# The recurrence's inputs, gate and value products moved beside the differential attention, with x loaded twice

## What is computed

```python
proj = x @ w_in            # columns a_q, a_f, a_i, a_g (512 each), b_q, b_k, b_v (512 each)
o_a = _hgrn2(a_q, a_f, a_i, lb)                 # 4 heads; scores (from q, f) times the inputs i
o_a = _rms_norm(o_a, hgrn_g) * silu(a_g)        # norm and gate of the recurrence
o_b = diff_attention(b_q, b_k, b_v, lam)        # 4 heads, (softmax(Q1K1') - lam softmax(Q2K2')) V
o_b = _rms_norm(o_b, diff_g) * (1.0 - lam_init)
x = LN(alpha * x + concat([o_a, o_b]) @ w_out)  # then SwiGLU; layer 1 is forgetting attention
```

## Time and profile before

| | us |
|---|---|
| median of 3 runs (lowest, highest) | 1513.64 (1512.14, 1517.49) |
| the profiled execution: its time | 1518.29 |
| the profiled execution: span, first to last instruction | 1516.5 |
| mean granted TensorE clock, share of full speed | 0.961 |
| PE busy | 1414.4 |
| DVE, ACT, POOL busy | 491.5, 499.5, 495.9 |

### The profile page before, as it was taken

One profiled execution on the slowest core, in us unless ns is written; L12 is line 12 of the kernel. 1 busy time (PEld: TensorE's weight loads), 2 busy tenths in 40 slices (PEclk: granted clock), 3 DMA queues, 4 the chain that ended last, 5 costly groups with the idle time before them and its releaser, 6 DMA issues.

```text
span 1516.5 us, 18942 instructions
## 1 busy us (share of the span) xinstructions
PE 1414.4 (93%) x7212; PEld 1182.7 (78%) x7212; DVE 491.5 (32%) x1120; ACT 499.5 (33%) x824; POOL 495.9 (33%) x213
## 2 busy tenths in 40 slices
PE   7999996798999999999989998889899999999997
PEld 5888874578888888877878887777679888888875
DVE  3366526554111111013636272542362111110105
ACT  4312335423323222112435554444423232322120
POOL 4421312033443535341242222202133344445340
PEclk9999997999999999999999999889899999999999
DMA  6211121021323233221232121012112323323211
GB/s 215 87 53 56 56 84 55 1 84 57 111 84 111 83 98 111 97 84 30 84 111 57 57 57 56 1 55 83 31 56 84 109 86 103 92 90 118 95 59 56
DMA packets 136322, 117.44 MB, mean 77 GB/s; under 512 B 5412, under 2 KB 112036, under 8 KB 136232
## 3 DMA queue, kind: packets, MB, share of 16 engines
q1 hardware_dynamic: 136232, 116.23, 24.6%
HBM read 114.12 MB, written 2.10 MB: 77 GB/s over the span
## 4 chain that ended last, share of the span: by engine, by line
PE 81%; DVE 8%; ACT 6%; issue 3%; DMA 1%; POOL 0%; ACTq 0%; POOLq 0%; DVEq 0%; SPq 0%
PE banks L448 24%; PE banks L450 23%; PE banks L449 23%; PE banks L851 2%; PE banks L869 2%; ACT w_hi L966 1%; PE banks L715 1%; PE banks L519 1%; ACT p_fox L1188 1%; PE banks L860 1%; DVE fox_ms L1496 1%; PE banks L815 1%; DVE o_even L1366 1%; DVE xT_lo L1240 1%; DVE small L1400 1%
## 5 line engine op out<-in xcount | busy, mean ns | idle before, releaser
L926 POOL TENSOR_TENSOR w_lo<-w_raw,w_hi 128x1024 fp32r<-128x1024 f32 (+1 forms) x209 | 495.7, 2393 | 983.9 <-ACT w_hi L966 983.9
L448 PE MATMUL banks<-xT_lo,w_hi 128*128 128x512 f32 (+2 forms) x912 | 345.4, 379 | 5.0 <-DVEq L1242 5.0
L449 PE MATMUL banks<-xT_hi,w_lo 128*128 128x512 f32 (+2 forms) x912 | 342.8, 376 | 0.0
L450 PE MATMUL banks<-xT_hi,w_hi 128*128 128x512 f32 (+2 forms) x912 | 342.7, 376 | 0.0
L966 ACT ACTIVATE w_hi<-w_raw 128x2048 fp32r<-128x2048 f32 (+1 forms) x107 | 200.0, 1869 | 215.5 <-PE banks L450 177.8
L448 PE MATMUL banks<-w_lo,xT_hi 128*128 128x512 f32 (+1 forms) x608 | 222.8, 366 | 9.9 <-issue 5.8
L450 PE MATMUL banks<-w_hi,xT_hi 128*128 128x512 f32 (+1 forms) x608 | 215.6, 355 | 0.0
L449 PE MATMUL banks<-w_hi,xT_lo 128*128 128x512 f32 (+1 forms) x608 | 215.3, 354 | 0.0
L448 PEld LDWEIGHTS banks<-xT_lo,w_hi 128*128 128x128 f32 (+1 forms) x912 | 173.1, 190 | 35.9 <-issue 5.8
L449 PEld LDWEIGHTS banks<-xT_hi,w_lo 128*128 128x128 f32 (+1 forms) x912 | 173.3, 190 | 30.4
L450 PEld LDWEIGHTS banks<-xT_hi,w_hi 128*128 128x128 f32 (+1 forms) x912 | 173.0, 190 | 30.7
(11 more groups left out here) (167 smaller groups left out, 1293.7 us busy)
## 6 DMA issues: line engine op xcount, KB each, us to landing
w_raw<-in_ffn_w_dram SPq DMA_DIRECT2D x92, 512.0 KB, 4.5
w_raw<-in_ffn_w_dram SPq DMA_DIRECT2D x20, 1024.0 KB, 4.9
w_raw<-in_fox_w_in_dram SPq DMA_DIRECT2D x16, 1024.0 KB, 5.8
w_raw<-in_even_w_in_dram SPq DMA_DIRECT2D x14, 1024.0 KB, 5.0
w_raw<-in_even_w_out_dram SPq DMA_DIRECT2D x4, 1024.0 KB, 5.0
w_raw<-in_fox_w_out_dram SPq DMA_DIRECT2D x4, 1024.0 KB, 6.7
x_res<-in_x_dram SPq DMA_DIRECT2D x4, 512.0 KB, 7.6
out_dram<-x_res SPq DMA_DIRECT2D x4, 512.0 KB, 2.6
```

The source lines that it names most:

```text
L448: mm(acc, l_hi, r_lo, start=first, stop=False)
L449: mm(acc, l_lo, r_hi, start=False, stop=False)
L450: return mm(acc, l_hi, r_hi, start=False, stop=final)
L926: ins = nc.gpsimd.tensor_tensor(w_lo[c % RING][:, a:a + n], w_raw[c % RAW][:, a:a + n], w_hi[c % RING][:, a:a + n].bitcast(F32), ALU.subtract)
```

## The change

The stage a_i leaves the mixed stretch, which keeps 24 pieces (b_q, b_k, b_v) and 40 units; the chunks of a_i are loaded after those of b_v. In the attention stretch 20 fillers stand in 16 slots: the 8 pieces of a_i, the value products of the 4 heads, the 8 pieces of a_g, filler k in slot k * 16 // 20. So a_i is in slots 0 to 5, the value products in slots 6, 7, 8 and 8, a_g in slots 9 to 15; slots 0, 4, 8 and 12 have two. The gate moves to slot 16, the turning to slot 18, and first_out behind the last slot. scT now holds all four heads. iv and a_gate lie in x_res, so x is loaded a second time (4 DMAs of 512 KB), ahead of the weights of out0[3], after all gate products.

```diff
-        mixed = [(c, p) for s in ("a_i", "b_q", "b_k", "b_v") for c in stage_chunks[s] for p in range(PIECES)]
+        mixed = [(c, p) for s in ("b_q", "b_k", "b_v") for c in stage_chunks[s] for p in range(PIECES)]
...
-        scT, e = take("scT", [2, 10, P], F32, e)
-        iv, e = take("iv", [NT, 512], F32, e)
+        scT, e = take("scT", [AH, 10, P], F32, e)
...
+        early = x_res[:, :, :].rearrange("p t n -> p (t n)").rearrange("p (a t n) -> p a t n", a=2, t=NT)
+        iv, a_gate = early[:, 0], early[:, 1]
...
-        gate_pieces = [(c, p) for c in stage_chunks["a_g"] for p in range(PIECES)]
-        GATE_AT = len(gate_pieces) + 1
-        TURN_AT = GATE_AT + 4
+        fillers = [("piece", c, p) for c in stage_chunks["a_i"] for p in range(PIECES)]
+        fillers += [("value", h, 0) for h in range(AH)]
+        fillers += [("piece", c, p) for c in stage_chunks["a_g"] for p in range(PIECES)]
+        FILL_SLOTS = D_UNITS
+        def fillers_at(s):
+            return [x for k, x in enumerate(fillers) if k * FILL_SLOTS // len(fillers) == s]
+        GATE_AT = FILL_SLOTS
+        TURN_AT = GATE_AT + 2
...   PE, slot s
+                for kind, a, b in fillers_at(s):
+                    if kind == "value":
+                        value_products(a)          # waits merge_done of the head and i_done, 4
+                    else:
+                        next(late[chunks[a][0]], None)
-                if TURN_AT + 2 <= s < TURN_AT + 2 + NT:
-                    next(first_out)
+                if s == TURN_AT:
+                    for t in range(NT):
+                        turn_tile("o0", t, o_even, lambda: pe.wait_ge(S["gated"], t + 1), t, (0,))
...   PE, behind the last slot
+            for t in range(NT):
+                pe.wait_ge(T_hi, 2 * NT + t + 1)
+                pe.wait_ge(T_lo, 2 * NT + t + 1)
+                next(first_out)
...   SP
+                if c == stage_chunks["out0"][3]:
+                    bank, count, _ = uses[("value", AH - 1)]
+                    sp.wait_ge(bank_full[bank], count)
+                    sp.wait_ge(S["gated"], NT)
+                    for t in range(NT):
+                        sp.dma_start(x_res[:, t, :], x[:, t, :]).then_inc(x_in[t], 16)
...   ACT, slot s, ahead of the exponentials
+                for kind, a, b in fillers_at(s - 1):
+                    if kind == "value":
+                        value_act(a)               # one evacuation, four squares
+                        continue
+                    if chunks[a][0] == "a_i" and a == stage_chunks["a_i"][1]:
+                        evac(("a_i", b), iv[:, b, :], whole)
+                        act.sem_inc(S["i_done"], 1)
+                    if b == 1 or b == PIECES - 1:
+                        hi_upto(a + 3 if b == 1 else a + 4)
+                for kind, a, b in fillers_at(s - 3):
+                    if kind == "value":
+                        root(stats[:, :, 16 + a], stats[:, :, 8 + a], S["var_hgrn"], a + 1, S["root_hgrn"])
...   ACT, slot s, behind the copy of unit s-2
+                if s == GATE_AT:
+                    for t in range(NT):
+                        evac(("a_g", t), a_gate[:, t, :], whole, ACT.Silu)
+                    act.sem_inc(S["gate_done"], 1)
+                    nc.scalar.preload_act_table_set(LN_EXP)
...   DVE, slot s, behind norm_head of the attention
+                for kind, h, _ in fillers_at(s - 2):
+                    if kind == "value":
+                        norm_var(h, 0)
+                for kind, h, _ in fillers_at(s - 4):
+                    if kind == "value":
+                        norm_head(h, 0)
+                if s == GATE_AT + 1:
+                    dve.wait_ge(S["gate_done"], 1)
+                    for t in range(NT):
+                        chain(tt(o_even[:, t, 0:512], o_even[:, t, 0:512], a_gate[:, t, :], ALU.mult), S["gated"])
```

More of the change, by code:

```diff
@@ L108, in weight_chunks @@
     columns("b_v", we, 3072)
+    columns("a_i", we, 1024)
     columns("a_g", we, 1536)
@@ L703, in unit_products @@
                 if kind in MM:
-                    acc = open_bank(("unit", u), 4 + nth((*MM, "value"), u) % 4, "dve")
+                    acc = open_bank(("unit", u), 4 + nth(MM, u) % 4, "dve")
                     pe.wait_ge(S["decayed"], nth(MM, u) + 1)
@@ L743, in _ @@
                 if stage not in pieces:
[L744 removed]
+                    if stage == "b_v":
                         pieces[stage] = columns(stage, "act")
@@ L749, in _ @@
                 next(pieces[stage], None)
-            for stage in ("a_i", "b_q", "b_k", "b_v"):
+            for stage in ("b_q", "b_k", "b_v"):
                 drain(pieces[stage])
@@ L778, in _ @@
                     n = (i + 1) * P
-                    maps = [open_bank(("score", s, m), (0 if wide and s % 2 else 4) + m, "act") for m in range(2)]
+                    maps = [open_bank(("score", s, m), 4 + m, "act") for m in range(2)]
                     for m, acc in enumerate(maps):
@@ L1010, in _, with value_act @@
             nc.scalar.preload_act_table_set(LN_EXP)
[L1012 to L1023 removed]
+            def value_act(h):
+                acc = full(("value", h))
+                release(fn(o_even[:, :, h * P:(h + 1) * P], acc[:, :].rearrange("p (t n) -> p t n", t=NT),
+                           ACT.Copy), ("value", h))
+                for t in range(NT):
+                    chain(fn(junk[:, :], o_even[:, t, h * P:(h + 1) * P], ACT.Square,
+                             accum_out=stats[:, t, 8 + h:9 + h]), S["ms_hgrn"] if t == NT - 1 else act_step)
             due = []
@@ L1373, in _ @@
                     merge(u - 2)
-                if u >= 6 and units[u - 6][0] == "value":
-                    norm_head(units[u - 6][1], 0)
             dve.sem_inc(S["act_free"], 1)
@@ L1415, in _ @@
                     norm_head(u // NT, 1)
-                if GATE_AT + 1 <= s <= GATE_AT + NT:
-                    t = s - GATE_AT - 1
-                    dve.wait_ge(S["gate_done"], 1)
-                    chain(tt(o_even[:, t, 0:512], o_even[:, t, 0:512], a_gate[:, t, :], ALU.mult), S["gated"])
+                for kind, h, _ in fillers_at(s - 2):
[5 more added lines that the diff above has]
+                if s == GATE_AT + 1:
+                    dve.wait_ge(S["gate_done"], 1)
+                    for t in range(NT):
+                        chain(tt(o_even[:, t, 0:512], o_even[:, t, 0:512], a_gate[:, t, :], ALU.mult), S["gated"])
+                if s == TURN_AT + 1:
+                    for t in range(NT):
+                        split_lo("o0", t, (0,))
             dve.sem_inc(S["o_ready"], NT)
             def add_left(key, t, half):
+                if key[0] == "out0" and half == 0:
+                    dve.wait_ge(x_in[t], 32)
                 xs = x_res[:, t, half * 512:(half + 1) * 512]
```

116 lines of the change are left out of this document (38 added, 78 removed).

## The result

| | before | after |
|---|---|---|
| median of 16 runs each (lowest, highest), us | 1514.63 (1510.2, 1517.68) | 1522.75 (1518.04, 1525.2) |
| the profiled execution: its time | 1518.29 | 1518.48 |
| its span | 1516.5 | 1516.7 |

The ratio is 1.0046, 95% interval 1.0035 to 1.0056: slower, where 1508.4 and faster were forecast, and outside the range of 1498 to 1520. Times are medians, and one kernel's runs spread over some 7 us. Two later sets of runs of the same kernel gave 1.0027 (1.0015 to 1.004) and 1.0035 (1.0023 to 1.0047). The two profiled executions are of nearly the same length only because that of before was among the longest of its kernel and that of after among the shortest; the stretches must be compared one by one.

The account below looks back on a forecast made before the run. PE was taken as the bound, busy 1414.4 of 1516.5 us, so a change gains only where PE waits. Terms -34.1 + 11.9 + 17.0 = -5.2 took the median 1513.6 to 1508.4 us, range 1498 to 1520.

Parts of the forecast that it names:

- the clock: Attention stretch: matmuls slowed by a lower granted clock, counted as 3 us in all.
- Mixed stretch: First unit to first filler: 8 pieces (22.9), 4 value products (8.6) and a wait (2.6) go, 34.1 us less.
- the wait of 3.18: Mixed stretch: PE's wait for DVE beside POOL was to go, with slower matmuls 2.6 us; bounds 0 and 4.
- Attention stretch: First filler to scores of unit 15: PE work 78.4 plus waits and clock, 90.5 against 78.6, 11.9 us more.
- slots 6 and 10: Attention stretch: value products wait 2.8 us for ACT's evacuation; unit 10's scores come 2.8 late behind ACT's value products.
- Slots 13 and 14: Attention stretch: five norm_heads on DVE, one beside POOL, delay unit 13's mix and maximum; 3.0 of 3.9 us counted.
- The end: Scores of unit 15 to out0[1]: the steps follow each other, 42.8 us instead of 25.8, 17.0 more.
- What costs nothing: Before out0[3]: the second load of x delays its weights, but they arrive at 35 and are rounded at 42.
- DVE is blocked more often: Attention stretch: four norm_heads meet POOL at 3.9 us each, 12.7 us more than the sum; 1521, slower; chance 0.18.
- the rival of the cover: Attention stretch: fillers cover the waits, 3 of 12.1 us of waits and clock stay; 1499; chance 0.17.
- Cancel: End at its upper bound (+4) and mixed-stretch stall back (+2.6): 1515, the same; chance 0.25.
- the other three: Signs of error: scores of unit 15 after 270, 5 us norm_heads more than once, PE waiting for w_hi of out0[3].

Follow-up runs that it names:

- the units moved by one piece: The changed kernel with the recurrence's units one weight piece later in the mixed stretch; 1519.58 us, ratio 1.0036.
- the repetitions: The changed kernel profiled and timed twice more with no edit; 1519.86 us (ratio 1.0027) and 1519.98 us (ratio 1.0035).
- the third: The third profile of the changed kernel, with no edit; 1519.98 us, ratio 1.0035.
- the run with no reload: The changed kernel without the second load of x, so its values are not the reference's; 1520.65 us, ratio 1.003.
- moving w_hi: The changed kernel with ACT rounding out0[1] in slot 14 instead of 13, so POOL starts behind the norm_heads; 1516.05 us, ratio 1.0004.
- The gate-first run: The changed kernel with Silu, gate products, turning and splitting earlier, and two first_out pieces between the last units' products; 1512.07 us, ratio 0.9979.
- two more edits: Added to the earlier gate: out0[1] rounded in slot 14, and value products one to a slot in two alternating banks; 1498.77 and 1497.85 us.

## Why the prediction was wrong

By its own terms: -34.1 + 11.9 + 17.0 = -5.2; the traces show -29.0 to -30.6, +17.3 to +17.5 and +16.4 to +16.5: +3.5 to +4.9. Two terms failed: the wait that was to go from the mixed stretch, and the price of DVE's collisions with POOL in the attention stretch. With them went the clock behind the waits.

**Mixed stretch, forecast 34.1, measured 29.0 to 30.6.** The 31.5 of matmuls for 8 pieces and 4 value products were about right. What failed is the 2.6 for the wait of 3.18, which I let go because DVE would have less to do. The trace of before had already spoken against that: DVE was idle for 1.03 us up to 127.46, just ahead of the two held operations, and the first norm_head of the value products came at 136.71, behind the wait. Nothing but POOL made DVE late. So the wait stayed, at 2.81, a new one of 0.93 came from the first widening, and the units moved by one piece brought it back at 3.04. The term's lower bound, 0, had the right mechanism ("another chunk meets the same place"); I chose the middle for no reason that a row gave. In place of 2.6 the term measured -0.9 in the first trace of after and -2.3 to -2.5 in the repetitions. The difference between these is clock: behind the same wait of 2.81, matmuls of 512 columns ran 0.43 us apart instead of 0.23 up to 137.3 in the first trace and up to 139.4 in the third. In the run with no reload, where no half clock followed that wait, the stretch is 32.1 shorter than before, and the term 0.6.

**Attention stretch, forecast 11.9, measured 17.3 to 17.5.** This is the step that failed most. The waits of slots 6 and 10 came at the places named and near the sizes named: 3.23 and 2.13 for 2.8 and 2.8. Slots 13 and 14 were forecast at 3.0. PE waited 5.66 there, not for the mix or the maximum but for the scaled copy of unit 9: 3.95 are the norm_head that POOL held, 1.71 stay without it. I took a part of the 3.9 us that one norm_head loses. It was lost whole, and the half clock behind it came on top, 5.6 to 5.8 in all, shown by moving w_hi. The wait of 1.11 for the mix of unit 0 was not forecast; POOL's widening of 180.56 made it. Summed by PE's rows: waits of 12.1 (1.11 + 3.23 + 2.13 + 5.66) where 9.1 were counted, and busy time of 83.5 where 78.4 + 3.0 were. For the clock I had 3 us in a lump; the rows show 1.7 at the first value products, 1.9 behind the wait of 2.13 and 1.8 behind that of 5.66.

**The end, forecast 17.0, measured 16.4 to 16.5.** This chain was right link by link, to within 0.5 us. From the scores of unit 15 (266.61): ACT's Silu done at 12.5 (276.59 + 2.48; forecast 12.5), table back at 13.8 (13.8), the gate products done at 19.8 (DVE, 283.50 + 2.87; forecast 19.8), the product of unit 15 begun at 21.0 (20.9), the first piece of first_out at 24.4 (24.7), the second turning at 37.0 (37.5), out0[1] at 42.3 (42.8). The gate-first run shows that 8.0 of the 16.5 were order and not need. The price of a change of table set was well taken from the trace: the load takes 1.28 and the next operation begins 0.01 to 0.02 behind it. The Trainium skill's 2.66 for a switch ("ScalarE: Activation LUTs", "What ACT_TABLE_LOAD costs") includes a drain that no row here shows.

**What costs nothing** was right: x was issued again at 286.46, 19.85 behind the scores of unit 15 (forecast 19.8), and leaving it out wins nothing.

**The rivals.** "DVE is blocked more often" forecast four blocked norm_heads. One was, and beside it the mixes of units 0 and 2, of which one cost PE 1.11 us and the other nothing; so its mechanism is there but not its count. The slot that both the forecast and the rival of the cover took as free of waits (226.03 to 230.75 before) had such a hold too: the mix in it took 1.77 and 2.42 us beside POOL (228.03 and 229.83), and PE had work meanwhile. A hold costs only what PE can't cover. The rival's 1521 is nearest to the first set's time, but that set lies 3 us above what the traces show. It said that it decides from the second collision on. In fact one, fully paid, a small one, and the one in the mixed stretch that did not go away were enough. "Cancel" was nearest in the trace, but for another reason: not the end, but the middle took the gain. The sign "mixed stretch shorter by less than 30" came in the repetitions (29.0 to 29.2; 30.6 in the first trace); the other three did not.

The Trainium skill ("SBUF — State Buffer", "SBUF: two separate sides") says that whichever engine starts first holds the shared port pair for its whole instruction. The traces agree: a held DVE operation took close to one POOL subtraction or what was left of it (1.4 to 2.7 us for one), and those that read PSUM, as 0.69 at 111.19 and 0.96 at 210.43 in the midst of a widening, took their usual time.

Priced whole from the rows of before, 3.9 for the norm_head instead of 3.0 and nothing for the wait in the mixed stretch, the forecast would have been -31.5 + 11.9 + 0.9 + 17.0 = -1.7, that is 1511.9. With the 5.7 that the collision cost with its clock, known only from the run with w_hi later, it is 0.1: no change. What the traces show beyond that (3.5 to 4.9) is for the most part the 0.93, the 1.11 and more half clock.

## What to carry to other kernels

Where two engines exclude each other, price a collision whole, with the wait that it causes, and don't count one as removed because the engine held has less to do. Look in the trace at what each start of the other engine will meet: moving that start moves the collision, and what counts is whether it lands where PE has work. Behind a PE wait of some 3 us allow for 0 to 3 us of matmuls at half clock, most often 1 to 2, wait by wait and not as a lump. When work is moved into the gaps of a chain, the tail behind the chain wants a new order in the same change: here the order of the gate alone was worth 7.8 us, where the loss was 4 to 8, and with two more edits the kernel with the moved work took 1.1% less time than before. Whether the same edits would have helped the kernel before without the move was not tested.

## What was not expected of the hardware

- A DVE operation of 4 columns (spans, 128x4) took 2.34 us, and one of 1 column (128x1) 1.92, beside POOL's subtraction. In these rows the hold does not depend on the size of what is held, so small operations of a chain are as exposed as large ones. Not every one is held: a reciprocal of 2 columns at 248.51, 0.3 us after POOL had begun, took its usual 0.17, and in after the statistics of x_res (128x512, 329.12 us) their usual 0.69 within a widening.
- The clock after the same wait is not the same from execution to execution: the same 20 matmuls, at 207.55 and 207.58 us behind the same wait of 3.23, took 2.47 in one and 4.10 in the other. The granted clock was 1.00 (2.4 GHz) in the one; in the other it was below 0.6, so that most of the 4.10 us ran at 1.2 GHz. Behind the same wait of 2.81 in the mixed stretch it made 3.2 us: 100.2 in one execution, 103.4 in another.
